# A decoder step on one core: the conditioning weights read in blocks of 128 rows by 1024 columns, with one turning per 1024 columns

## The reference

```python
def trunk(x, c, ...):
    cs = jax.nn.silu(c)                       # 9 rows in all, 2048 wide
    for i in range(DEPTH):                    # 2 layers
        mod = cs @ ada_w[i] + ada_b[i]        # ada_w[i]: 2048 x 12288
        sh1, sc1, g1, sh2, sc2, g2 = jnp.split(mod, N_ADA, axis=-1)
        h = rmsnorm(x, norm_mix_g[i]) * (1.0 + sc1[:, None]) + sh1[:, None]
        ...                                   # layer 0: retention, 8 heads; layer 1: pooling mixer
        x = x + g1[:, None] * out
        h = rmsnorm(x, norm_ffn_g[i]) * (1.0 + sc2[:, None]) + sh2[:, None]
        x = x + g2[:, None] * swiglu(h, ffn_w_in[i], ffn_w_out[i])
    return rmsnorm(x, final_norm_g), ...
```

## Time and profile before

| what | value |
|---|---|
| time, 3 runs | 3436.25, 3438.39, 3441.3 us; median 3438.39 |
| the profiled execution | its own time 3435.37 us, span 3433.3 us, granted TensorE clock 0.979 in the mean |
| busy | PE 97%, PEld 90%, DVE 50%, ACT 32%, POOL 4% |
| chain that ended last | PE 88%, DMA 5%, DVE 4% of the span |
| loads of ada_w into the ring | 128 of 512 KB, median 6.1 us from issue to landing |
| loads of w_in (heads) into the ring | 192 of 512 KB, median 6.2 us |
| loads of the feed-forward's first weight | 352 of 512 KB, median 3.6 us |

### The profile page before, as it was taken

One profiled execution on the slowest core, in us unless ns is written; L12 is line 12 of the kernel. 1 busy time (PEld: TensorE's weight loads), 2 busy tenths in 40 slices (PEclk: granted clock), 3 DMA queues, 4 the chain that ended last, 5 costly groups with the idle time before them and its releaser, 6 DMA issues.

```text
span 3433.3 us, 55153 instructions
## 1 busy us (share of the span) xinstructions
PE 3313.4 (97%) x23867; PEld 3094.5 (90%) x23867; DVE 1713.8 (50%) x2680; ACT 1092.6 (32%) x1354; POOL 135.2 (4%) x174
## 2 busy tenths in 40 slices
PE   7899999999999988999999999999799999999998
PEld 4688888989888878999999999999799999999998
DVE  3234564635446358444444444444845555555554
ACT  2232323323322223333333333333533333333334
POOL 0000000000000011000000000001300000000001
PEclk8899999999999999999999999999899999999999
DMA  9776868677686856777777777775244444444443
GB/s 324 256 240 197 258 202 266 193 250 237 211 273 200 267 199 203 242 230 233 233 230 230 233 233 229 231 229 165 68 150 151 148 152 149 149 153 148 151 150 105
DMA packets 627892, 701.17 MB, mean 204 GB/s; under 512 B 21150, under 2 KB 590943, under 8 KB 627322
## 3 DMA queue, kind: packets, MB, share of 16 engines
q1 hardware_dynamic: 606016, 619.26, 56.1%
q0 software_dynamic: 20544, 75.02, 6.9%
q10 hardware_dynamic: 1090, 3.38, 0.3%
HBM read 656.10 MB, written 41.48 MB: 203 GB/s over the span
## 4 chain that ended last, share of the span: by engine, by line
PE 88%; DMA 5%; DVE 4%; ACT 1%; issue 1%; SPq 0%; POOL 0%; ACTq 0%; DVEq 0%; POOLq 0%
PE pair L1453 76%; DMA sb_raw<-in_ada_w 3%; PE adab L1491 3%; PE adab L1466 2%; PE m L1433 1%; DMA sb_raw<-in_ret_w_in 1%; DVE sb_w_lo L924 1%; DVE sb_big L1268 1%; PE m L1731 1%; PE m L1697 1%; PE m L1503 1%; DMA sb_o_s<-in_ada_w 1%; PE pair L1433 0%; DMA sb_big<-in_ada_w 0%; DVE sb_X L1050 0%
## 5 line engine op out<-in xcount | busy, mean ns | idle before, releaser
L924 DVE TENSOR_TENSOR sb_w_lo<-sb_raw,sb_w_hi 128x1024 fp32r<-128x1024 f32 x792 | 964.8, 1222 | 1264.2 <-ACT sb_w_hi L611 1258.8
L611 ACT ACTIVATE sb_w_hi<-sb_raw 128x1024 fp32r<-128x1024 f32 x792 | 838.2, 1059 | 1869.9 <-PE pair L1453 1514.2
L1453 PE MATMUL pair<-sb_h_hi,sb_w_hi 128*128 128x320 f32 x4480 | 1038.7, 313 | 16.5 <-DVE sb_h_lo L1032 7.3
L1453 PE MATMUL pair<-sb_h_lo,sb_w_hi 128*128 128x320 f32 x4480 | 1026.0, 310 | 0.0
L1453 PE MATMUL pair<-sb_h_hi,sb_w_lo 128*128 128x320 f32 x4480 | 1025.5, 310 | 0.0
L1453 PEld LDWEIGHTS pair<-sb_h_hi,sb_w_hi 128*128 128x128 f32 x4480 | 750.6, 189 | 39.6 <-issue 31.7
L1453 PEld LDWEIGHTS pair<-sb_h_hi,sb_w_lo 128*128 128x128 f32 x4480 | 754.0, 189 | 0.0
L1453 PEld LDWEIGHTS pair<-sb_h_lo,sb_w_hi 128*128 128x128 f32 x4480 | 753.9, 189 | 0.0
L1453 PE MATMUL pair<-sb_y_hi,sb_w_hi 128*128 128x320 f32 x1856 | 429.8, 313 | 6.4 <-DVE sb_y_lo L1256 6.4
L1453 PE MATMUL pair<-sb_y_lo,sb_w_hi 128*128 128x320 f32 x1856 | 424.5, 310 | 0.0
L1453 PE MATMUL pair<-sb_y_hi,sb_w_lo 128*128 128x320 f32 x1856 | 424.2, 310 | 0.0
(11 more groups left out here) (257 smaller groups left out, 1584.8 us busy)
## 6 DMA issues: line engine op xcount, KB each, us to landing
sb_raw<-in_ffn_w_in SPq DMA_DIRECT2D x352, 512.0 KB, 3.6
sb_raw<-in_ret_w_in SPq DMA_DIRECT2D x192, 512.0 KB, 6.2
sb_raw<-in_ffn_w_out SPq DMA_DIRECT2D x176, 512.0 KB, 3.4
sb_big<-in_ada_w SPq DMA_DIRECT2D x168, 512.0 KB, 5.0
sb_raw<-in_ada_w SPq DMA_DIRECT2D x128, 512.0 KB, 6.1
sb_big<-in_state_ret POOLq DMA_DIRECT2D x32, 1024.0 KB, 8.1
sb_raw<-in_ret_w_out SPq DMA_DIRECT2D x64, 512.0 KB, 4.2
out_state_ret_sample<-sb_big POOLq DMA_DIRECT2D x32, 1024.0 KB, 5.9
```

The lines of the kernel that those rows point to most:

```text
L611: A(w_hi[s][:, :, :], raw[slot][:, :, :], ACT.Copy).then_inc(hi_done, 1)
L924: V.tensor_tensor(w_lo[s][:, :, :], raw[slot][:, :, :], w_hi[s][:, :, :].bitcast(F32), ALU.subtract)\
L1453: ins = MM(pair[p][:, m, 0:T], w[s][:, k, P * m:P * m + P], x[:, c, :], start=first and k == 0 and n == 0, stop=last and k == BK - 1 and n ...
```

## The change

A block of ada_w is now 128 rows by 1024 columns (512 KB as before). Its four matmuls have the same stationary operand, 128 rows of csT, and take four stretches of 256 columns, so each column group gathers its own columns over 16 blocks. Sixteen blocks make a group of 1024 columns; ScalarE copies the bank once per group (128 x 256), TensorE turns it in 2 matmuls against `pick`, which has 36 columns and keeps the column groups apart, and VectorE adds the bias for 8 x 9 columns at once. There are 20 such groups: one per head, and 12 in the feed-forward of layer 0, where eight blocks are still taken every 11 gemms and the copy, turning and bias follow every second time. In a head the copy is in the gate lap after its third split, the turning stands after step E, ahead of the gate lap, into `mbank[2]`, and the take after step E on VectorE; the group of head 0 is turned in head 1 ahead of the K/Q lap. Step F waits for the take, as its bank is the same. Head 0 has no ring blocks in its V lap; it has eight in the K/Q lap and eight in the gate lap. ScalarE's `take_mod` and its semaphore are gone; VectorE waits for the takes with `taken`.

```diff
-    halves = [False, True] + [True] * 3 + [False] + (head + none) * (H - 1) + none
+    halves = none + [True] * 4 + (head + none) * (HEAD_GROUPS - 1) + none * 4 * (H - HEAD_GROUPS) + none
...
-        tab[c::KPAD, C_FOLD + c] = 1.0
+        for j in range(4):
+            tab[KPAD * j + c, C_PICK + NC9 * j + c] = 1.0
...
+            def ada_rows(n, k):
+                layer, chunk = group_at(n)
+                return a["ada_w"][layer][P * k:P * k + P, P * chunk:P * chunk + 4 * BN]
...
-                load_block(block_of(w_in, 512 * k, VCOL + BN * j), 0 if k >= 2 else None)
+                load_block(block_of(w_in, 512 * k, VCOL + BN * j))
...
-                sp.dma_start(eight[e], block_of(a["ada_w"][1], 512 * (i % 4), BN * (2 * g + i // 4))).then_inc(eight_in[e], 16)
+                sp.dma_start(eight[e], ada_rows(HEAD_GROUPS + n, k)).then_inc(eight_in[e], 16)
...
+            def copy_group():
+                act.wait_ge(ada_done, PRE_BLOCKS + C("group", 1) * DC)
+                ...
+                A(ada_sb[:, :], adab[:, 0:BN], ACT.Copy).then_inc(ada_copied, 1)
...
+            def take_group(src):
+                dve.wait_ge(ada_folded, C("group", 1))
+                ...
+                V.tensor_tensor(mods[layer][:, chunk:chunk + 8, :].rearrange("p (j c) n -> p c j n", c=2), ...
+                                bias.unsqueeze(3).broadcast_to([P, 2, 4, NC9]), ALU.add).then_inc(mod_dve, 1)
...
+            def ada_block(block):
+                k = C.n["ada"] % DC
+                if k == 0 and groups():
+                    pe_.wait_ge(ada_copied, groups())
                 for j in range(4):
-                    ins = MM(adab[KPAD * j:KPAD * j + KPAD, 0:BN], csT[:, 4 * k + j, :],
-                             raw[s][:, j, :], start=k == 0, stop=k == 3)
+                    ins = MM(adab[KPAD * j:KPAD * j + KPAD, 0:BN], csT[:, k, :], block[:, BN * j:BN * j + BN],
+                             start=k == 0, stop=k == DC - 1)
...
+            def fold_group(bank):
+                pe_.wait_ge(ada_copied, C("folds", 1))
+                pe_.wait_ge(mod_dve, C("folds", MOD_PRE))
                 for c in range(2):
-                    ins = MM(bank[:, NC9 * c:NC9 * c + NC9], ada_sb[:, P * c:P * c + P], fold, start=True, stop=True)
+                    at = 4 * NC9 * c
+                    ins = MM(bank[:, at:at + 4 * NC9], ada_sb[:, P * c:P * c + P], pick, start=True, stop=True)
...
             def eights_beside():
-                if eights_due(C.n["gemm"], 1):
-                    fold_eight()
+                if (eight_due(C.n["gemm"], 1) or 0) % 2:
+                    fold_group(mbank[C.n["folds"] % 2])
...
             def head(free=True, last=False):
+                group = C.n["head"] < HEAD_GROUPS
                 step_A(free)
-                lap16(step_B, ada=True)
+                lap16(step_B, ada=group)
                 step_C()
-                lap16(step_D, ada=True, beside=True)
+                lap16(step_D, ada=group, fold=C.n["head"] == 1)
                 step_E()
-                lap16(step_F, beside=True)
+                if group:
+                    pe_.wait_ge(ac["D"], C("head"))
+                    fold_group(mbank[2])
+                lap16(step_F)
...
-            ada_block(), ada_block()            # after first_gemm(6) and after first_gemm(7)
-            lap16(ada=True, beside=True)
-            lap16(ada=True, beside=True, halves=1)
+            lap16(ada=True)
+            lap16(ada=True)
```

More of the change, by code:

```diff
@@ L57 @@
 NC9 = 1 + NS
[L58 to L59 removed]
+PRE_STRIPS, PRE_SLOTS = 8, 6
 PRE_BLOCKS = 8 * PRE_STRIPS
@@ L324, in _, with load @@
         def _(sp):
-            C = Counts("unit", "gemm", "ada", "adas")
+            C = Counts("unit", "gemm", "ada", "owed")
             recent = []
-            def load(kind, src):
+            def load(kind, src, wide=False):
                 s = C.n["unit"] % RAW_SLOTS
@@ L338, in load, with load_block @@
                 C.n[kind] += 1
-            owed = []
-            def load_block(src, ada=None, now=False):
+            def load_block(src, ada=False):
                 assert C.n["unit"] == gemm_place[C.n["gemm"]]
@@ L347, in load_block, with load_ada, load_k16 @@
                     return
[L348 to L357, removed]
+                for _ in range(C.n["owed"]):
+                    load_ada()
+                C.n["owed"] = 2 * int(ada)
+            def ada_rows(n, k):
+                layer, chunk = group_at(n)
+                return a["ada_w"][layer][P * k:P * k + P, P * chunk:P * chunk + 4 * BN]
+            def load_ada():
+                n, k = divmod(C("ada", -PRE_BLOCKS), DC)
                 assert C.n["unit"] == ada_place[C.n["ada"]]
[L359 to L363, removed]
+                load("ada", ada_rows(n, k), wide=True)
+            def load_k16(w, cols, ada=False):
                 for n in range(8):
-                    load_block(block_of(w, 512 * (n % 4), cols[n // 4]), ada, now=end and n == 7)
+                    load_block(block_of(w, 512 * (n % 4), cols[n // 4]), ada)
             def load_k4(w, row):
@@ L401, in _ @@
                     load_first(g + 1)
-            load_k16(w_in, [KCOL, QCOL], ada=0)
-            for n in range(8):
-                load_block(block_of(w_in, 512 * (n % 4), GCOL + BN * (n // 4)), 0 if n < 4 else None)
+            load_k16(w_in, [KCOL, QCOL], ada=True)
+            load_k16(w_in, [GCOL, GCOL + BN], ada=True)
             head(1, True)
@@ L582, in _ @@
         def _(act):
-            C = Counts("gemm", "adas", "head", "y")
+            C = Counts("gemm", "group", "head", "y")
             A = nc.scalar.activation
@@ L612, in split, with lap @@
                 C.n["gemm"] += 1
-            def copy_ada():
-                act.wait_ge(ada_done, C("adas") * 4 + 4)
-                if C.n["adas"] == ADA0:
+            def copy_group():
+                act.wait_ge(ada_done, PRE_BLOCKS + C("group", 1) * DC)
+                if C.n["group"]:
+                    act.wait_ge(ada_folded, C("group"))
+                else:
                     act.wait_ge(pre_folded, PRE_STRIPS)
-                else:
-                    act.wait_ge(ada_folded, C("adas", -ADA0))
                 A(ada_sb[:, :], adab[:, 0:BN], ACT.Copy).then_inc(ada_copied, 1)
[L622 to L639, removed]
+                C.n["group"] += 1
+            def lap(posts, copy=False, ahead=0):
                 for k in range(8):
@@ L643, in lap @@
                         split()
[L644 to L647, removed]
+                    if k == 2 and copy:
+                        copy_group()
+                    if (eight_due(C.n["gemm"], 4) or 0) % 2:
+                        copy_group()
                     for post in posts.get(k, ()):
@@ L905, in _ @@
         def _(dve):
-            C = Counts("gemm", "adas", "head", "y", "step")
+            C = Counts("gemm", "group", "head", "y", "step")
             V = nc.vector
@@ L1168, in rotate @@
                 dve.wait_ge(gemm_done, C("gemm", back))
-                take_mod(pair[j][:, 0, T:T + 2 * NC9], step=1 if j == 0 else 3)
+                if j == 0 and C.n["head"] == 1:
+                    take_group(pair[0][:, 0, T:])
                 for half, (f0, f1, op) in enumerate(((cos, sin, ALU.subtract), (sin, cos, ALU.add))):
@@ L1427, in _ @@
         def _(pe_):
-            C = Counts("gemm", "ada", "adas", "folds", "strip", "head", "y")
+            C = Counts("gemm", "ada", "folds", "strip", "head", "y")
             MM = nc.tensor.matmul
@@ L1497, in fold_eight @@
[L1497 to L1505 removed]
             def eights_beside():
[L1509 removed]
+                if eight_due(C.n["gemm"]) is not None:
```

161 lines of the change are left out of this document (62 added, 99 removed).

## The result

The changed kernel took 3383.18 us (median of 4 runs, 3378.42 to 3387.04) beside 3437.32 us for the kernel before on the same chip: a ratio of 0.984, with a 95% interval of 0.9823 to 0.9857. That is 54.1 us less, where 43.8 were forecast. The profiled execution took 3381.22 us, with a span of 3379.4 and a granted clock of 0.984 in the mean, so both profiled executions lie within 3 us of their medians and can be compared stage by stage.

A forecast was written before the change was run, and what follows sets the result against it. TensorE, busy 97% of the span, was taken as the bound, so its own list counts in most stages. Savings 14.2 + 7.0 + 2.8 + 8.3 + 6.5 + 5 = 43.8 us from 3438.39 gave 3395 us, range 3380 to 3412.

The forecast's parts named there:

- the rival "more": Bigger pieces clear the waits, head 0's K/Q and gate laps giving 10.5 us, heads 1 to 7 13.6: 3382; 13%.
- part 5: K/Q and gate lap of head 0: 70.0 us against 76.5, 6.5 us won, bounds 0 and 10.5.
- part 6: Waits for ada blocks in heads 1 to 7, 13.6 us: 4 KB pieces win 5, bounds 0 and 13.6.
- Part 4: From first V lap to K/Q lap: of 11.79 us only one gemm of 3.53 stays, 8.3 us won.
- the rival "less at the start": Head 0 needs 286 GB/s, leaving little room to absorb waits; K/Q-gate laps and ada waits give nothing: 3406; 28%.
- Parts 1 and 2: Fewer turnings: 14.2 us removed in the first feed-forward, 7.0 us in heads 1 to 7.
- so 0.40 per group: First feed-forward: each new turning of 4 instructions, 36 columns wide, at 0.10 us each; bounds 0.39 to 0.44.
- 3 x 0.35 + 0.54: Heads 1 to 7: the turnings before, 1.59 us per head, of which one of 0.54 stays.
- Part 3: End of early ada_w loads: without ring blocks in the first V lap early blocks come 2.8 us sooner, at most 7.6.

The follow-up runs named there:

- the moved version: Changed kernel with state loads shifted by one gemm off gemms after which SP issues ada block pairs: 3370.70 us, again 3369.93 beside the changed kernel's 3382.70.
- the run with the early loads alone: Kernel before with SP issuing the first two ring ada_w blocks after the last early block, turnings kept: 3432.13 us against 3436.11, ratio 0.9984.

## Why the prediction was right, and where it was off

The measured 3383 lies within the 3380 to 3412 of the prediction, but 3 us under the forecast's own 3386 to 3402 and within 2 us of the 3382 of the rival "more". That closeness is chance. The rival wanted 10.5 us from part 5 and 13.6 from part 6; they gave 6.7 and 5.1. The 10.1 us beyond the forecast are 3.9 in the turnings, 1.8 in the early loads (0.8 of it already there at 102 us), 0.3 in parts 5 and 6, and 4.1 that no part had.

*Part 4* came out as worked out: the K/Q lap starts 8.3 us closer to the fifth gemm. *Part 5* came out in size. The two laps of head 0 take 69.74 us for a forecast of 70.0, 66.0 of work and about 4 of waiting. Of the 4, 1.99 are one wait for a block at 191.98, and 8.77 - 7.23 = 1.54 are the 48 matmuls behind it, where the granted clock was 0.81 in the mean. The prediction had counted on no such slow stretch in these laps, so half of its 4 is right by luck. Wait and slow stretch stand behind one meeting (a state load at 181.49, the pair at 181.81), and in the moved version the laps follow one another at 7.23 per pair of gemms. That the rival "less at the start" did not come is shown by the second execution of the same version: 148.00 to 210.60 there moves 292 GB/s with the engines 0.89 busy, and TensorE waits for a block once, 0.40 us, so the share that this rival feared was not a limit.

```profile
148.00:210.60 62.60, 62.20 (x484) 56.00 (x477) 24.19 (x35) 15.23 (x16) 2.34 (x3) 1.00 0.89 292
```

*Parts 1 and 2, the turnings, were sized too small*, 21.2 forecast for 25.1. The step that failed is "so 0.40 per group" and "3 x 0.35 + 0.54" as the whole price. The prediction itself read that the switch from ada blocks back to gemms costs 0.19 and did not ask the same of a turning. The kernel before and the changed one, each with the state loads moved, show it where neither waits. Step A of two heads in a row, before and then changed:

```profile
813.21 1.47 PE L1677 MATMUL m<-sb_qT,sb_kT 128*128 128x256 f32 x8
...
958.97 1.47 PE L1677 MATMUL m<-sb_qT,sb_kT 128*128 128x256 f32 x8
```

```profile
495.94 1.47 PE L1634 MATMUL m<-sb_qT,sb_kT 128*128 128x256 f32 x8
...
640.34 1.47 PE L1634 MATMUL m<-sb_qT,sb_kT 128*128 128x256 f32 x8
```

145.76 against 144.40, 1.36 per head, not 1.05. And the chains of the two, around one place where a turning went:

```profile
705.34 1.72 PE m L1697 x4
707.05 0.35 PE pair L1479 x4
707.40 7.14 PE pair L1453 x48
```

```profile
678.22 1.72 PE m L1654 x4
679.94 7.04 PE pair L1424 x48
```

The 48 matmuls behind a turning take 0.10 longer: 3 x (0.35 + 0.10) = 1.35. In the feed-forward the same: the gemms lose 3.72 + 35.29 - 38.92 = 0.09 where the turning is gone, and the turning that stays takes 0.37, not 0.40. So width was free (the four instructions of 36 columns cost less than four of 9), and the count of interruptions was worth more than their busy time.

*Part 3* was taken at its lower bound, 2.8, and came out a little above it. The wait for the early block fell by 2.77 (6.42 to 3.65). Counted from the early block at 102 us on, the fifth gemm moved up by 3.8 us in the changed kernel and by 3.35 in the run with the early loads alone. The prediction took the DMA engines for full from their share of 115 to 131 us. Just ahead of that, behind SP's stand, they were not; the same stretch before and after (columns as in the earlier trace rows):

```profile
113.00:116.00 3.00, 0.00 (x0) 0.00 (x0) 1.49 (x1) 2.31 (x4) 0.00 (x0) 1.00 0.92 278
```

```profile
113.00:116.00 3.00, 0.94 (x8) 0.20 (x8) 0.74 (x1) 1.49 (x2) 0.00 (x0) 0.71 1.05 378
```

The 100 GB/s missing there for 3 us are 0.3 MB. As a block of 0.524 MB came every 1.40 us, I estimate them at 0.8 us, which with the 2.8 makes 3.6.

*Part 6* has the right size (5.1 us against 5) and names only a part of the cause. The 5.1 are a remainder; the waits for ring blocks in heads 1 to 7 fell by 3.4 (12.8 to 9.4). The prediction set the packets of the two queues against each other. The Trainium skill, in "DMA: Bandwidth & Descriptors", section "Queues, rings and completion order", has each engine go round its queues packet by packet. By that rule, with the packets of the earlier trace rows put in, the prediction let most of 13.6 us go. The same section of the Trainium skill counts about 9 to 17 descriptors to a packet, while the rows come to one packet for each 1.0 KB, so the prediction's shares of the engine do not follow from the section alone. The runs agree with the direction: 1 KB pieces in the changed kernel bring 16.1 us of waits, 4 KB pieces 11.3. That is a third of 13.6, and with the state loads moved both sizes of the changed kernel wait for 0.4 us or less. Nearly all waits stand where a state load is issued within a microsecond of a pair of blocks, which has about two gemms (7.06 us) to land; the piece only sets how much such a meeting costs. The row was there to be seen: the earlier trace rows have the state load at 683.69 and the block at 684.45. The prediction named the two times and priced the packets. The rival "more", in which bigger pieces clear the waits, falls for the same reason.

A meeting costs more than its wait, too. Moving the state loads took 10.1 us of waits and 12.8 us of time out of the changed kernel, and 12.7 of waits and 19.8 of time out of the kernel before; the stretch of 8.77 after a wait of 1.99 shows one part of the rest. The remainder of the 19.8 I have not traced to rows; the two profiled spans of the kernel before are 16.3 apart (3433.3 and 3417.0). It also divides the gain anew: with the state loads moved in both, the change is worth 3416.68 - 3369.93 = 46.8 us, so about 7 of the measured 54.1 are meetings that the change made cheaper.

*What stays open* are the 4.1 us that no part forecast. One row shows 1.2 of them: the 60 matmuls at the end of the first feed-forward, before and after.

```profile
2359.92 11.69 PE pair L1453 x60
```

```profile
2309.37 10.45 PE pair L1424 x60
```

They follow a gap in TensorE's work in both, and ran slower before. But the same 60 matmuls took 9.06 us in the trace of the kernel before with its early loads moved, and 11.83 in that of the changed kernel with 1 KB pieces, so the change is not shown to be the cause, and I give none for the 4.1.

## What to carry to other kernels

Price an interruption of a matmul stream by what it does to the stream, not by its own busy time: compare the stream's piece with and without it in the chain of waits (here 0.10 us on top of 0.35). Where two queues have loads on a schedule, lay their issue times side by side before you ask about bandwidth or packets: one gemm's shift of the loads was worth 12.8 and 19.8 us here, at the same bytes. And a fix that makes a collision cheaper hides the fact that the collision can be avoided; test with the collision gone.

## What the runs showed of the hardware

Two executions of one and the same kernel (the moved version) had spans of 3375.7 and 3361.9 us, and all but 0.6 us of the difference lies in a few stretches where TensorE has thin work: the heads (1000.6 in both), the eights of the first feed-forward (989.9 and 989.7) and the second feed-forward (936.9 and 936.5) agree. The same 22 us in both, from 126 us on (length, busy PE, PEld, DVE, ACT, POOL, clock, DMA share, GB/s):

```profile
126.00:148.00 22.00, 21.50 (x128) 21.15 (x125) 7.70 (x10) 10.06 (x20) 0.00 (x0) 0.82 0.42 128
```

```profile
126.00:148.00 22.00, 22.00 (x158) 21.57 (x161) 8.84 (x11) 11.11 (x21) 0.00 (x0) 1.00 0.43 132
```

In the first the six gemms take 23.62 us, a part of it at 1.2 of the 2.4 GHz (granted clock 0.50 from 128.60 to 133.40), in the second 21.22. By head 1 the two are 4.3 us apart (210.9 and 206.6), by the first eight blocks of the feed-forward 7.8, and by the second feed-forward 13.4. So a stage of 2 to 5 us in a single profiled execution can be the clock, and the medians over runs have to carry such a claim.

A state load on GpSimd's queue and a pair of blocks on SP's, issued 0.3 us apart (655.70 and 656.04), gave the second block a landing of 8.75 us, where TensorE reached it after 7.73 (665.26 - 1.06 - 656.47). Issued one gemm apart, the same loads cost TensorE no wait in one execution of the moved version and one of 0.4 us in the other, with the DMA engines 0.89 busy from 148.00 to 210.60.
